# Staging places for the down units and the last two up units of a mixture-of-experts kernel, and up loads in pairs

## Chip, cores and metric
One core of a Trainium2 chip (trn2) runs one program. The metric is the time of one execution on the device in microseconds (us). The engines are TensorE (PE in the profile), VectorE (DVE), ScalarE (ACT), GpSimd (POOL) and SyncE (SP), which only issues DMAs; 16 DMA engines move the data.

## What is computed
One inference step of a decoder layer over 528 prompt rows (16 meta tokens and 512) and 8 sample rows of width 1024, float32: a gated linear attention group and a sliding-window attention group, their output projection, then a mixture of experts and a last RMS norm. The change is in the experts, cut to what matters:

```python
def moe_ffn(x2d, w_router, b_router, w_up, b_up, w_down, b_down):
    logits = (x2d @ w_router) + b_router                   # 520 tokens, 32 experts
    top_v, top_e = lax.top_k(logits, TOP_K)                # 4 experts per token
    gates = jax.nn.softmax(top_v, axis=-1)
    # tokens are grouped by expert and padded to whole blocks
    def expert_block(args):
        xb, e = args
        hh = xb @ w_up[e] + b_up[e]                        # (block, 1024) @ (1024, 2048)
        return clamped_swiglu(hh) @ w_down[e] + b_down[e]  # (block, 1024) @ (1024, 1024)
    # the results, times their gates, are added to each token
```

An expert's weights are 8 MB (up) and 4 MB (down). Every expert is read once.

## The kernel before
**Stages.** Until about 325 us the kernel projects, runs both attention groups and the router, and takes the products of the first block. The rest is the block loop and a tail that sums up each token's four expert outputs.

**Blocks.** Rows of one expert are cut into blocks of `SUB` = 64. With these inputs there are 46 blocks; 14 of the 32 experts have two, which stand one behind the other (blocks 0 and 1 are expert 0's). A table made on the chip orders the experts so that those with two blocks are spread, and holds for each block its expert and whether it is the expert's first (`is_new`).

**Units.** The weights come in units of 128 x 2048 float32 (1 MB): `UPU` = 8 for up, `DNU` = 4 for down. The tile `raw` has 12 places; unit j lies in place `SLOT[j]`, so there is one place for each unit of an expert. Four more places, `ahead`, take the first four ups of the second expert at the start; the region is work space otherwise.

**SyncE** issues all loads of weights in program order (lines 595 to 777). Before a unit's load it waits until TensorE has used that unit in the block before: `up_used` counts up units, `dn_used` down units. A load of a repeated block is issued with a false condition: nothing moves, its semaphore rises. In the loop over b from 4 (line 733) it issues the eight ups of block b (line 604) and then the four downs of block b - 1 (line 614). The loads of blocks 0, 2 and 3 are written out ahead of the loop (lines 674 to 731). Behind the loop come the last block's downs (line 747), then, once all but the last two blocks are scattered, `t_small` (line 741) and the eight `slot_pair` loads of the expert outputs (line 760).

**TensorE** does `up(b)` and then `down(b - 1)` (line 2317). `up_products` (line 2154) is four products per unit, two column halves by two banks; `down` (line 2273) the same for a down unit. At the start the order is written out: second_up (block 1), three units of third_up (block 2), down(0), one unit, down(1), `place` (which makes the lists of rows and outputs on TensorE), four units, then block 3.

**VectorE** clamps, forms SwiGLU and turns rows to columns with 32 x 32 transposes. Around 340 to 366 it makes `own_pos`, `dest`, `at_slot`, `at_block` and the lists from them, and then raises `lists_ready` (line 1537).

**ScalarE**, per block (line 1048), in order: `sigmoid(b)`, `seed_up(b + 1)` (the up biases into two PSUM banks), `hold(b + 2)` (gathered rows to `x_hold`), `y_out(b - 1)` (the down bank to `y_rows`), `seed_down(b)`. **GpSimd** gathers rows and scatters outputs by indirect DMAs.

**The tail.** TensorE's `small_slots` (line 2342) waits for `t_small`, then come `pair_rows` of four tiles, `rest_slots(2)`, `pair_rows(4)` and `rest_slots(4)` (line 2325), all in order. VectorE weighs the loaded slots (line 1756), adds TensorE's sums (line 1764) and multiplies by the gain `g_final_bc` (line 1744), which is loaded at line 731.

## Time and profile before
| what | us |
|---|---|
| median of 3 runs | 1339.25 (1336.02 to 1340.25) |
| span of the profiled execution | 1337.8 |
| TensorE busy (matmul) | 1283.2, 96% of the span |
| VectorE busy | 918.0, 69% |
| ScalarE busy | 285.1, 21% |
| SyncE's queue: moved | 441.56 MB, 81.2% of 16 engines' span |
| all DMA packets | 468.95 MB, mean 351 GB/s |

The profile is of one execution; times in it are microseconds from the first instruction. A matmul record counts as busy from its issue to a modelled end, so a TensorE that waits shortly between units still looks nearly full. The granted TensorE clock is 0.995 of 2.4 GHz in the mean, so nothing here is about the clock. A wait is given with what ended it. "PE ps L2159" is TensorE's work at line 2159 (a line of `up_products`) that writes PSUM.

### The profile page before, as it was taken

To read this page: it belongs to the slowest core of one execution; us is meant where nothing else is said; L and a number is where in the kernel's file an instruction comes from. 1 tells how busy PE (TensorE), PEld (TensorE's weight loads), DVE (VectorE), ACT (ScalarE), POOL (GpSimd) and SP (SyncE) were. 2 spreads that over 40 slices of the span, in tenths; PEclk is the share of its full clock that TensorE was granted. 3 is DMA by queue.
4 is the path that set the end of the run, shared out by engine and by line. 5 is a ranking of instruction groups with operands and counts; after the bars stand their busy time and mean duration, and the time that the engine had idled before them with its cause. 6 is when DMAs were issued, how large, how long until landed. Compare 5 with 4: busy or idle time off the path is not lost.

```text
span 1337.8 us, 21359 instructions
## 1 busy us (share of the span) xinstructions
PE 1283.2 (96%) x6323; PEld 520.2 (39%) x6323; DVE 918.0 (69%) x1877; ACT 285.1 (21%) x542; POOL 124.1 (9%) x229
## 2 busy tenths in 40 slices
PE   8999999999999999997999998899999997999996
PEld 6876565553333333332333332233333331333332
DVE  3215357656878777775787786687777875777778
ACT  4331143433112121111121121111121111121114
POOL 2000000000020110100110101010111100110100
PEclk9998999999999999999999999999999999999999
DMA  9405154078999999999999999999999999999996
GB/s 358 129 4 191 32 176 170 32 284 342 417 386 386 421 421 419 416 421 421 420 398 423 414 422 420 414 422 407 420 417 420 414 421 421 421 402 420 412 414 274
DMA packets 91409, 468.95 MB, mean 351 GB/s; under 512 B 11870, under 2 KB 29520, under 8 KB 41074
## 3 DMA queue, kind: packets, MB, share of 16 engines
q1 hardware_dynamic: 75070, 441.56, 81.2%
q0 software_dynamic: 7360, 16.79, 3.2%
q10 hardware_dynamic: 8948, 10.19, 2.2%
q8 instruction: 19, 0.31, 0.1%
q14 instruction: 12, 0.10, 0.0%
HBM read 614.82 MB, written 28.77 MB: 481 GB/s over the span
## 4 chain that ended last, share of the span: by engine, by line
PE 71%; DMA 21%; DVE 4%; SPq 2%; issue 1%; ACT 0%; DVEq 0%; POOL 0%; POOLq 0%; ACTq 0%
PE ps L2159 34%; DMA raw<-in_w_down_dram 19%; PE ps L2284 17%; PE ps L1845 5%; PE ps L1822 5%; PE ps L2060 3%; SPq L614 1%; DMA raw<-slot_outputs 1%; PE ps L2173 1%; DVE v_gate L1756 1%; DMA x_rows<-expert_inputs,row_idx 1%; PE ps L1924 0%; PE ps L2007 0%; PE ps L2015 0%; PE ps L2014 0%
## 5 line engine op out<-in xcount | busy, mean ns | idle before, releaser
L2159 PE MATMUL ps<-raw,xT 128*64 128x512 f32 x2816 | 617.4, 593 | 17.6 <-DMA raw<-in_w_up_dram 17.0
L1632 DVE STREAM_TRANSPOSE xT<-x_hold 32x192 f32<-32x192 f32 (+2 forms) x680 | 275.0, 404 | 154.1 <-PE ps L2159 133.9
L2159 PEld LDWEIGHTS ps<-raw,xT 128*64 128x64 f32 x2816 | 199.9, 137 | 424.6 <-issue 391.0
L2284 PE MATMUL ps<-raw,aT 128*64 128x512 f32 x1408 | 317.1, 595 | 16.7 <-DMA raw<-in_w_down_dram 16.7
L1632 DVE STREAM_TRANSPOSE aT<-act_g 32x256 f32<-32x256 f32 x352 | 223.5, 635 | 64.4 <-PE ps L2284 54.5
L2284 PEld LDWEIGHTS ps<-raw,aT 128*64 128x64 f32 x1408 | 97.6, 137 | 229.2 <-issue 174.7
L1016 ACT ACTIVATE act_s<-act_g 128x512 f32<-128x512 f32 x46 | 29.0, 630 | 632.6 <-DVE act_g L1616 632.6
L566 POOL DMA_INDIRECT slot_outputs<-y_rows,out_idx x44 | 45.2, 1028 | 609.3 <-ACT y_rows L1021 608.4
L1404 DVE STREAM_TRANSPOSE bias_up<-up_cols 128x1024 f32<-128x1024 f32 x46 | 57.3, 1245 | 1.6
L1845 PE MATMUL ps<-w_c_cols,hT 128*128 128x512 f32 x128 | 56.8, 596 | 0.0
L558 POOL DMA_INDIRECT x_rows<-expert_inputs,row_idx x47 | 49.3, 1049 | 71.2 <-issue 53.5
L1021 ACT ACTIVATE y_rows<-ps 128x512 f32<-128x512 f32 x45 | 26.9, 597 | 99.0 <-PE ps L2284 99.0
L2060 PE MATMUL ps<-w_out_sb,mixT 128*128 128x512 f32 x96 | 42.8, 599 | 0.1
L1012 ACT ACTIVATE x_hold<-x_rows 128x512 f32<-128x512 f32 x45 | 28.3, 630 | 59.6 <-DVE xT L1632 58.5
L1616 DVE TENSOR_SCALAR act_g<-ps 128x512 f32<-128x512 f32 x46 | 31.8, 692 | 10.8 <-PE ps L2159 9.5
L1822 PE MATMUL ps<-hT,w_a_cols 128*128 128x268 f32 x160 | 36.6, 390 | 0.0
L1845 PEld LDWEIGHTS ps<-w_c_cols,hT 128*128 128x128 f32 x128 | 23.7, 190 | 27.8 <-issue 27.8
L1623 DVE TENSOR_TENSOR act_g<-act_l,act_s 128x512 f32<-128x512 f32 x46 | 31.8, 692 | 1.6
L1621 DVE SCALAR_TENSOR_TENSOR act_l<-act_l,act_g 128x512 f32<-128x512 f32 x46 | 31.8, 692 | 1.4
L966 ACT ACTIVATE ps<-bias_up 128x512 f32<-128x512 f32 x47 | 28.3, 601 | 20.8 <-DVE bias_up L1404 13.8
L1822 PEld LDWEIGHTS ps<-hT,w_a_cols 128*128 128x128 f32 x160 | 30.3, 190 | 6.1 <-issue 0.4
L1617 DVE TENSOR_SCALAR act_l<-ps 128x512 f32<-128x512 f32 x46 | 31.3, 681 | 0.0
(405 smaller groups left out, 899.7 us busy)
## 6 DMA issues: line engine op xcount, KB each, us to landing
raw<-in_w_up_dram SPq DMA_DIRECT2D x356, 1024.0 KB
raw<-in_w_down_dram SPq DMA_DIRECT2D x180, 1024.0 KB, 10.5
slot_outputs<-zeros ACTq DMA_DIRECT2D x1, 8320.0 KB, 27.9
...
```

The lines of the kernel that those rows point to most:

```text
L558: pool.indirect_dma_start(x_rows[:], None, xn_halves, bass.IndirectOffsetOnAxis(ap=idx[:, 0:1], axis=0), bounds_check=last_row, oob_is_err ...
L566: pool.indirect_dma_start(slot_halves, bass.IndirectOffsetOnAxis(ap=out_idx[:, 0:1], axis=0), y_rows[:], None, bounds_check=last_out, oob_ ...
L1404: return dve.transpose(bias_up[:].rearrange("p a (c r) -> p (a c) r", r=32), bc(up_cols[:], 2, [P, 2 * COLS, 32]))
L1616: dve.tensor_scalar(act_g[:], ps[:, banks[0], :], LIMIT, None, ALU.min).then_inc(g_ready, 1)
L1621: o.do(dve.scalar_tensor_tensor(act_l[:], act_l[:], 1.0, act_g[:], ALU.add, ALU.mult))
L1623: dve.tensor_tensor(act_g[:], act_l[:], act_s[:], ALU.mult).then_inc(a_ready, 1)
L1632: dve.transpose(dst_at(rows_out, group), src_at(rows_in, parity)).then_inc(done, 1)
L1822: ins = mm(ps[:, n % 4, 0:HALF], w[:, k, c0:c0 + P], hT[:, k, half], start=(k == 0), stop=(k == KT - 1))
L1845: ins = mm(ps[:, bank, 0:n], hT[:, k, a:z], w[:, k, c0:c0 + n], start=(k == 0), stop=(k == KT - 1))
L2060: ins = mm(ps[0:r, 6 + n, :], mixT[:, k, 0:r], w_out_sb[:, k, 512 * n:512 * n + 512], start=(k == 0), stop=(k == KT - 1))
L2159: ins = mm(ps[SUB * i:SUB * i + SUB, banks[bank], :], rows_in[:, j, :], weights[:, c:c + HF], start=False, stop=(j == at_end), skip_group_ ...
L2284: ins = mm(ps[SUB * i:SUB * i + SUB, 2, :], aT[:, j, r, :], raw[:, units[j], D * r + HF * i:D * r + HF * i + HF], start=False, stop=(j == ...
```

## The change
- The places. There are 18 instead of 16: 12 low ones, and six high ones (`HIGH`) where other tiles lay. Each unit has a home (`UP_AT`, `DOWN_AT`); ups 6 and 7 and the four downs have a staging place too (`UP_STAGE_AT`, `DOWN_STAGE_AT`). Tiles of the stages before and of the tail move accordingly; `own_pos`, `dest`, `at_slot` and `at_block` now lie in `LATE0` to `HIGH1`, which are the staging places of downs 2 and 3.
- ScalarE gets `move_ups` (two copies of 128 x 2048 per block) and `move_downs` (four), each from the staging place to the home once TensorE has used the home's last content; for a repeated block the source is the home itself.
- SyncE loads a staged unit once its staging place is emptied (`up_moved`, `down_moved`), and ups 0 to 5 as before, once TensorE has used them. Ups are loaded in pairs of units, the staged pair first. The table has two rows more, from which SyncE takes the blocks to wait for (`block_ahead`, `previous_start`); `is_new` becomes a two-bit value.
- TensorE waits for a copy (`up_moved`, `down_moved`) instead of a landing for the staged units. Its order of work is the same, but for the order of units in the first three blocks and `up(3)`, `down(2)`, now inside the loop.
- At the start, the second expert's two staged ups and downs 0 and 1 are loaded ahead; its downs 2 and 3 after `lists_ready`; its home ups by `load_ups(2)`.
- At the end, the last block's downs are used from the staging places, and `t_small` and `g_final_bc` are loaded behind the eight slot loads.

The diff, cut to its core:

```diff
-AHEAD = 4
-BY_LANDING = list(range(AHEAD, UPU)) + list(range(AHEAD))
+BY_LANDING = [3, 2, 0, 1, 4, 5, 6, 7]
+STAGED = (UPU - 2, UPU - 1)
...
+        LOW = [RAW0 + UNIT * 4 * i for i in range(UPB)]
+        HIGH = [HIGH0 + UNIT * 4 * i for i in range(6)]
+        UP_AT = [HIGH[0], HIGH[1], LOW[10], LOW[11], LOW[0], LOW[1], LOW[2], LOW[3]]
+        UP_STAGE_AT = [LOW[5], LOW[6]]
+        DOWN_AT = [LOW[4], LOW[9], HIGH[2], HIGH[3]]
+        DOWN_STAGE_AT = [LOW[7], LOW[8], HIGH[4], HIGH[5]]
+        SLOTS_AT = UP_STAGE_AT + UP_AT[0:6]
...
+        def staged_or_home(stage, home, new):
+
+            low, step = min(stage, home) // 4, abs(stage - home) // 4
+            which = new if stage > home else 1 - new
+            return weights[:, low:low + 2 * step].rearrange("p (k s) -> p k s", k=2)[:, bass.ds(which, 1), 0:UNIT]
...
+        R = Region(LATE0, HIGH1)
         own_pos = R("own_pos", [P, NTILE, NE])
         dest = R("dest", [P, NTILE, TOPK])
         dest_slot = R("dest_slot", [P, NTILE, TOPK])
         dest_block = R("dest_block", [P, NTILE, TOPK])
...
+            def load_up_pair(e, j, cond):
+                at = UP_STAGE_AT[0] if j in STAGED else UP_AT[j]
+                sp.sem_inc(weights_asked, 1)
+                sp.dma_start(unit(at, 2), up_source(e, j, 2), cond=cond).then_inc(landed[j], 16)
...
-                    load_up(0, 0, None)
-                    load_up(0, 1, None)
+                    load_first(3)
+                    load_first_down(1)
                     sp.wait_ge(max_ready, PT)
-                    load_up(0, 2, None)
+                    load_first(2)
                     sp.wait_ge(pv_psum, PT)
-                    load_up(0, 3, None)
-                    for j in range(AHEAD):
-                        load_ahead(1, j, None)
+                    load_first(0)
+                    load_first(1)
+                    load_first_down(2)
+                    load_first_down(3)
+                    load_second(STAGED[0])
                     sp.wait_ge(mixT_psum, 2 * NTILE)
-                    load_up(0, 4, None)
+                    load_second(STAGED[1])
                     sp.wait_ge(out_psum, NTILE)
-                    for j in range(5, UPU):
-                        load_up(0, j, None)
+                    for j in range(4, UPU):
+                        load_first(j)
...
+            load_first_down(0)
             sp.wait_ge(part_psum, NTILE)
             sp.wait_ge(h2_stored, 16 * NTILE)
             sp.wait_ge(caches_stored, 2 * 16)
-            for j in range(2, DNU):
-                load_down(0, j, None)
+            load_second_down(0)
+            load_second_down(1)
...
+            def load_ups(b):
+                e_up, new = expert(sp, b), is_new(sp, b)
+                ahead, previous = block_ahead(sp, b), previous_start(sp, b)
+                sp.wait_ge(landed[STAGED[0]], 16 * b)
+                sp.sem_inc(weights_asked, 1)
+                sp.wait_ge(up_moved, 2 * previous + 2)
+                load_up_pair(e_up, STAGED[0], new // 2)
+                for j in range(0, STAGED[0], 2):
+                    sp.wait_ge(landed[j], 16 * b)
+                    sp.sem_inc(weights_asked, 1)
+                    sp.wait_ge(up_used, UPU * ahead + (j + 2))
+                    load_up_pair(e_up, j, new % 2)
+
             def load_downs(b):
-                e_dn, new_dn = expert(sp, b - 1), is_new(sp, b - 1)
+                e_dn, new, previous = expert(sp, b), is_new(sp, b), previous_start(sp, b)
                 for j in range(DNU):
-                    sp.wait_ge(dn_used, DNU * b + (j + 1))
-                    load_down(e_dn, j, new_dn)
+                    sp.wait_ge(landed[UPU + j], 16 * b)
+                    sp.sem_inc(weights_asked, 1)
+                    sp.wait_ge(down_moved, DNU * previous + (j + 1))
+                    load_down(e_dn, j, new // 2)
 
             sp.wait_ge(table_made, 1)
-            e_up, new_up = expert(sp, 2), is_new(sp, 2)
-            other = second_is_other(sp)
-            sp.wait_ge(ahead_landed, AHEAD_LANDED + 16 * AHEAD)
-            for n, j in enumerate(range(AHEAD, UPU)):
-                sp.wait_ge(up_used, UPU + n + 1)
-                load_up(e_up, j, new_up)
-                if n < AHEAD:
-                    sp.sem_inc(landed[n], 16)
-                    load_ahead(e_up, n, other)
-            e_up, new_up = expert(sp, 3), is_new(sp, 3)
-            for n, j in enumerate(range(AHEAD)):
-                sp.wait_ge(up_used, 2 * UPU - AHEAD + n + 1)
-                load_up(e_up, j, None)
-            for n, j in enumerate(range(AHEAD, UPU)):
-                sp.wait_ge(up_used, 2 * UPU + n + 1)
-                load_up(e_up, j, new_up)
-            load_downs(3)
-            sp.wait_ge(up_used, 3 * UPU)
-            sp.dma_start(g_final_bc[:], g_final.rearrange("(a n) -> a n", a=1).to_broadcast([P, D])).then_inc(ld_gfinal, 16)
             nb = block_count(sp)
+            sp.wait_ge(second_landed, SECOND_LANDED + 4 * 16)
+            load_ups(2)
+            sp.wait_ge(lists_ready, 1)
+            load_second_down(2)
+            load_second_down(3)
+            load_ups(3)
+            sp.wait_ge(second_landed, SECOND_LANDED + 6 * 16)
+            load_downs(2)
             with sp.Fori(4, nb) as b:
-                e_up, new_up = expert(sp, b), is_new(sp, b)
-                for j in range(UPU):
-                    sp.wait_ge(up_used, UPU * b + (j + 1 - UPU))
-                    load_up(e_up, j, new_up)
-                load_downs(b)
+                load_ups(b)
+                load_downs(b - 1)
...
             def load_last_down(e, j):
-                src = w_down[0, column(e)].rearrange("a (p c r) n -> c p (a r n)", c=DNU, r=2)[j]
-                sp.wait_ge(up_used, UPU * sent + (UPU + j + 1))
-                sp.dma_start(raw[:, LAST_DOWN[j], :], src).then_inc(last_down_landed[j], 16)
-
-            def unit_is_free(j):
-                if j < UPU:
-                    sp.wait_ge(up_used, UPU * sent + (UPU + j + 1))
-                else:
-                    sp.wait_ge(dn_used, DNU * nb + (j - UPU + 1))
+                sp.wait_ge(down_moved, DNU * ahead + (DNU + j + 1))
+                sp.dma_start(unit(DOWN_STAGE_AT[j]), down_source(e, j)).then_inc(last_down_landed[j], 16)
...
-            load_small()
             for n in range(len(SLOT_ORDER)):
                 load_slots(n)
+            sp.wait_ge(dn_used, DNU * sent + 3 * DNU)
+            load_small()
+            sp.dma_start(g_final_bc[:], g_final.rearrange("(a n) -> a n", a=1).to_broadcast([P, D])).then_inc(ld_gfinal, 16)
...
+            def move_ups(b):
+                new = is_new(act, b) % 2
+                act.wait_ge(landed[STAGED[0]], 16 * b + 16)
+                for i, j in enumerate(STAGED):
+                    act.wait_ge(up_used, UPU * b + (j + 1 - UPU))
+                    act.activation(unit(UP_AT[j]).unsqueeze(1), staged_or_home(UP_STAGE_AT[i], UP_AT[j], new),
+                                   ACT.Copy).then_inc(up_moved, 1)
+
+            def move_downs(b):
+                new = is_new(act, b) % 2
+                for j in range(DNU):
+                    act.wait_ge(landed[UPU + j], 16 * b + 16)
+                    act.wait_ge(dn_used, DNU * b + (DNU + j + 1))
+                    act.activation(unit(DOWN_AT[j]).unsqueeze(1), staged_or_home(DOWN_STAGE_AT[j], DOWN_AT[j], new),
+                                   ACT.Copy).then_inc(down_moved, 1)
+
             act.wait_ge(table_made, 1)
             nb = block_count(act)
             act.wait_ge(up_read, 2)
             seed_up(3, (0, 1))
+            move_ups(2)
+            y_out(1)
+            move_downs(2)
             sigmoid(2)
             act.wait_ge(up_read, 3)
+            seed_down(2)
+            move_ups(3)
             hold(4)
-            y_out(1)
-            seed_down(2)
-            with act.Fori(3, nb) as b:
+            last = scattered_blocks(act)
+            with act.Fori(3, last) as b:
                 sigmoid(b)
                 act.wait_ge(up_read, b + 1)
                 seed_up(b + 1, (0, 1))
+                move_ups(b + 1)
                 hold(b + 2)
                 y_out(b - 1)
                 seed_down(b)
+                move_downs(b)
...
+            def up_landed(j, b):
+                if j in STAGED:
+                    pe.wait_ge(up_moved, 2 * b + (j - STAGED[0] + 1))
+                elif j % 2 == 0:
+                    pe.wait_ge(landed[j], 16 * b + 16)
...
+            def down(b):
+                pe.wait_ge(down_seeded, b + 1)
+                pe.wait_ge(aT_ready, 8 * b + 8)
+                for j in range(DNU):
+                    pe.wait_ge(down_moved, DNU * b + (j + 1))
+                    down_products(j, aT, unit(DOWN_AT[j]))
...
+            third_up(range(0, 3))
+            first_down(0, aT)
+            third_up(range(3, 4))
+            first_down(1, aT_last)
             place()
-            third_up(BY_LANDING[4:])
+            third_up(range(4, UPU))
             pe.wait_ge(table_made, 1)
             nb = block_count(pe)
-            up(3)
-            down(2, aT, SLOT[UPU:])
-            with pe.Fori(4, nb) as b:
+            with pe.Fori(3, nb) as b:
                 up(b)
-                down(b - 1, aT, SLOT[UPU:])
+                down(b - 1)
             turn_small()
```

## Rows read from the trace of the kernel before

**Rows 1.** Page, section 2: GB/s in 40 slices of 33.4 us, whole span.
```profile
GB/s 358 129 4 191 32 176 170 32 284 342 417 386 386 421 421 419 416 421 421 420 398 423 414 422 420 414 422 407 420 417 420 414 421 421 421 402 420 412 414 274
```

**Rows 2.** Page, section 4: chain that ended last, by engine.
```profile
PE 71%; DMA 21%; DVE 4%; SPq 2%; issue 1%; ACT 0%; DVEq 0%; POOL 0%; POOLq 0%; ACTq 0%
```

**Rows 3.** Waits of TensorE: who waited for whom, us in total, times, longest.
```profile
PE ps L2159 <- DMA raw<-in_w_up_dram: 17.0, 24, 1.3
```

**Rows 4.** Timeline, TensorE, 616 to 680: start, us, operation, idle before and releaser.
```profile
618.96 1.94 PE L2159 MATMUL ps<-raw,xT 128*64 128x512 f32 x8 [0.56 <-DMA raw<-in_w_up_dram]
...
633.16 13.90 PE L2159 MATMUL ps<-raw,xT 128*64 128x512 f32 x64
...
653.76 13.90 PE L2159 MATMUL ps<-raw,xT 128*64 128x512 f32 x64
```

**Rows 5.** Windows: busy us of PE, PEld, DVE, ACT, POOL, PEclk, DMA share, GB/s.
```profile
320.00:340.00 20.00, 19.42 (x101) 7.58 (x103) 15.95 (x43) 5.89 (x12) 1.00 (x1) 1.00 0.75 289
370.00:380.00 10.00, 10.00 (x48) 3.31 (x46) 8.20 (x15) 2.35 (x4) 3.35 (x5) 1.00 0.82 306
405.00:420.00 15.00, 15.00 (x74) 5.01 (x72) 13.57 (x27) 3.58 (x6) 2.27 (x3) 1.00 0.90 340
420.00:1320.00 900.00, 865.59 (x3960) 280.12 (x3957) 675.19 (x1315) 154.72 (x262) 98.18 (x160) 1.00 1.01 417
690.00:705.00 15.00, 14.46 (x68) 4.44 (x66) 11.41 (x23) 3.58 (x6) 2.28 (x4) 1.00 0.96 372
1320.00:1325.00 5.00, 5.00 (x13) 2.25 (x12) 4.74 (x6) 2.87 (x5) 0.00 (x0) 1.00 0.22 92
```

**Rows 6.** Windows, the same columns: 4 KB rows (25:35), 8 KB rows (662:682).
```profile
25.00:35.00 10.00, 10.00 (x45) 8.21 (x44) 0.00 (x0) 5.63 (x8) 0.73 (x4) 1.00 1.02 422
662.00:682.00 20.00, 20.00 (x96) 6.67 (x94) 16.24 (x32) 3.58 (x6) 2.45 (x4) 1.00 1.01 420
```

**Rows 7.** Timeline, SyncE's queue, 327 to 344: start, us of issuing, load, count.
```profile
329.39 0.34 SPq L604 DMA_DIRECT2D raw<-in_w_up_dram  x1
...
335.74 6.12 SPq L601 DMA_DIRECT2D raw<-in_w_up_dram  x4
343.43 12.32 SPq L604 DMA_DIRECT2D raw<-in_w_up_dram  x4
```

**Rows 8.** Timeline, VectorE's lists and TensorE's first products of block 3.
```profile
364.37 0.23 DVE L1531 TENSOR_SCALAR lst<-ps 128x68 f32<-128x68 f32 x1 [0.75 <-PE ps L2210]
...
365.49 0.23 DVE L1536 SCALAR_TENSOR_TENSOR row_idx_all<-lst 128x68 int32<-128x68 f32 x1
...
371.02 2.32 PE L2159 MATMUL ps<-raw,xT 128*64 128x512 f32 x10
```

**Rows 9.** Groups of ScalarE by form: count, busy us, mean ns, idle before.
```profile
L1016 ACT ACTIVATE act_s<-act_g 128x512 f32<-128x512 f32 x46 | 29.0, 630 | 632.6 <-DVE act_g L1616 632.6
...
L1080 ACT ACTIVATE t_sq<-v_gate 128x1024 f32<-128x1024 f32 x4 | 4.2, 1057 | 6.0 <-DVEq L1765 4.0 <-DVEq L1759 2.0
```

**Rows 10.** SyncE's line 604, not-done loads, then done: ns min/median/max, first, last.
```profile
L604 SPq DMA_DIRECT2D raw<-in_w_up_dram x8: 73/73/88, 608.2 to 623.7; - x8
...
L604 SPq DMA_DIRECT2D raw<-in_w_up_dram x8: 332/333/346, 656.7 to 668.0; - x8
```

**Rows 11.** Timeline from 1291: SyncE, then TensorE, then VectorE of the tail.
```profile
1291.95 0.81 SPq L741 DMA_DIRECT2D t_small<-slot_outputs  x2
...
1312.61 1.04 PE L2346 MATMUL ps<-t_small,small_hitT 32*24 32x512 f32 x4
1313.97 7.44 PE L2337 MATMUL ps<-y_pair,t_hitT 128*128 128x512 f32 x16 [0.33 <-ACT y_pair L1070]
...
1324.68 3.60 PE L2330 MATMUL ps<-raw,t_diag 128*128 128x512 f32 x8
...
1330.43 1.22 DVE L1764 TENSOR_TENSOR v_gate<-ps,v_gate 128x1024 f32<-128x1024 f32 x1
...
1333.45 1.28 DVE L1744 SCALAR_TENSOR_TENSOR v_gate<-v_gate,t_stat,g_final_bc 128x1024 f32<-128x1024 f32 x1
```

282 lines of the change are left out of this document (151 added, 131 removed).

## The prediction

> **What bounds the kernel now.** I read the slices first: from the eleventh of 40 to the last but one the 16 DMA engines move 386 to 423 GB/s, mostly about 421 [rows 1]. The chain of waits then names TensorE for 71% of the span and DMA for 21% [rows 2], which looks like a TensorE kernel. The waits correct that: TensorE's up line waits 24 times for weights, 17.0 us in sum [rows 3], and the busy share hides more. Where TensorE is starved, a unit (1 MB, eight matmul records) starts every 2.49 us though it is busy 1.94; where it is not, blocks of 8 up and 4 down units start 20.60 us apart (633.16 and 653.76), 1.72 a unit [rows 4]. 1.049 MB in 2.49 us is 421 GB/s. So the block loop has two rates that lie close together. TensorE needs 20.6 us for a block; DMA needs 12 x 2.49 = 29.9 us for an expert. There are 46 blocks (the sigmoid runs 46 times [rows 9]) over 32 experts, so 14 blocks reuse their expert's weights; 43 blocks lie between the start of block 3 at 371.0 [rows 8] and the end, 22.1 us each. 43 x 20.6 = 886 us would fit into 926. **The bound is the stream of bytes**: with it at 417 GB/s over 900 us [rows 5], the time can only fall by filling holes in the stream, and rises by every new hole. All is reckoned as "where does the stream end": now at 1321.1 (the window 1320:1325 moves 92 GB/s, 1.1 us of full flow [rows 5]), where the last of the eight slot loads lands; the end of the span, 1337.8, is 16.7 us behind it.
>
> **Holes of now.** Against 421, window 320:340 (289) lacks 6.3 us, 370:380 (306) 2.7 and 405:420 (340) 2.9; 420:1320 (417) lacks 8.6, most of it in small dips where a repeated block holds the places, such as 690:705 (372, 1.7 us) [rows 5]. Sum 20.5 us: this is all that staging can win, since bytes stay the same.
>
> **Part 1, staging in the loop.** Before, a unit's load waits until TensorE has used the unit in the block before. After, six of twelve units land in a staging place that is free as soon as ScalarE has moved the last content, also during a repeat. In a full stream the next expert's first home pair is asked for after 4 downs, 4 downs and a staged pair (25 us), and TensorE needs 17 for what must be used by then (four up units, four downs, two ups of the repeat: 10 x 1.72). So the holes at 370:380 and 405:420 (5.6 us) go, and of the 8.6 us I take 5 (bounds 0 and 8.6: window 690:705 has a DMA share of 0.96, not of 0.88 as its bytes would have, so part of the loss is small gather and scatter packets, which stay [rows 5]).
>
> **Part 2, the copies.** Six per block, 128x2048, SBUF to SBUF, also for a repeat (home onto home). Nearest rows: 128x512 takes 630 ns, 128x1024 1057 ns, both SBUF to SBUF [rows 9], so 0.83 ns an element and 2048 give 1.91 us. Bounds: 1.9, and 2.5 if the address in a register or in-place reading costs as much as a whole small instruction. ScalarE has 3.58 us of work in a block now (six instructions in 662:682 [rows 6]); with 11.5 it has 15.1 of 20.6. The up copies lie behind the seeding of the next block, in the 6.9 us of down products; the down copies behind the seeding of the down bank, in the 13.7 us of the next up products. Queued behind them on ScalarE is the next sigmoid, for which VectorE waits, and then the seeds, for which TensorE waits. If downs land late, ScalarE stands in `move_downs`, and seeds come some 1 to 2 us after the last down product instead of before it. That makes TensorE late, not the stream: cost 0, covered by the 40 us that TensorE has over. SyncE's extra register loads and waits (about 2 us a block) have the same cover; a load that is not done holds SyncE for only 73 ns against 332 [rows 10], so repeats pass through.
>
> **Part 3, loads in pairs.** Rows of 16 KB where there were 8 KB, and 2 MB per load. Is the stream faster? The `w_c_cols` load has rows of 4 KB and its window 25:35 runs at 422; the 8 KB rows in 662:682 run at 420 [rows 6]. Doubling the row brought nothing there, so I take 0 (bounds: 1% either way on the some 600 us of up loads that remain, 6 us). The Trainium skill ("DMA: Bandwidth & Descriptors", section Why small descriptors are slow) gives a fixed overhead of about 3 cycles per packet, beside 256 cycles for 8 KB. By it the up loads would win an estimated 0.6%, some 3.5 us; the two windows show nothing of it.
>
> **Part 4, the start, where the change loses.** Both kernels ask for 16 units before the block table is made, at nearly the same times. Before, SyncE then feeds the stream without a pause: block 2's last four ups from 327.4 (the second at 329.39), block 3's first four from 335.74, its others from 343.43, and then block 2's downs [rows 7]. After, block 2's staged ups and two downs are there already; its six home units come in pairs as units 1, 3 and 5 of block 1 are used, the first at 329.4, the last near 337. With a microsecond from issue to flow (an estimate) they move from 330.5 to 345.5. Then **SyncE stands at `lists_ready`**, because downs 2 and 3 of the second expert land where `own_pos`, `at_slot` and `at_block` lie until the lists are made, and block 3's eight ups, free to load, are queued behind it. VectorE ends the lists at 365.7; it idled 0.75 us before their first row [rows 8]. The table gets some seven small operations more, of about 0.2 us like the lists' own, 1.3 us in sum; less the 0.75 that is 366.3. Flow starts at 367.8. Holes: 323.2 to 330.5 is 7.3, 345.5 to 367.8 is 22.3, in sum 29.6, against 6.3 in 320:340 now. Block 3's first pair lands after two downs, the staged pair and itself, at 367.8 + 6 x 2.49 = 382.7; TensorE, ready at 371.0 [rows 8], stands 12 us. From there on the stream is full: SyncE's next wait, for `move_ups(3)` (behind four down copies that start near 376, the sigmoid, a seed and itself, 7.6 + 1.2 + 3.8), ends near 389, and the stream has work until 392.
>
> **Part 5, the tail.** The final gain vector and the small slots are loaded behind the eight slot loads instead of at 371 and at 1291.95 [rows 11]. That takes 0.66 MB out of the stream before its measured end: -1.5 us. But `small_slots` is the first of TensorE's last products, and all that follows stands behind it. Now it starts at 1312.61, 8.5 us before the stream ends; the four pair products follow at 1313.97 for 7.44, the last `rest_slots` runs 1324.68 for 3.60 [rows 11]. After, it starts when `t_small` has landed, 1.5 us behind the slots (bounds 0.5 and 3: completion of a small load). From its start to the end of the last product it is 1324.68 + 3.60 - 1312.61 = 15.7, then from VectorE's add 1330.43 to its last product's end 1333.45 + 1.28 = 1334.7 another 4.3 [rows 11], and 3.1 to the end of the span. VectorE alone comes to about the same: it has three tiles done, then tile 3 (5.2), norm, two adds, two norms, add; I take 0.2 more. Sum 1.5 + 15.7 + 4.3 + 3.1 + 0.2 = 24.8 behind the stream's end, where it is 16.7 now: **+8.1**. The loads of the last downs and slots have their places earlier than now; that is worth nothing in a full stream.
>
> **Sum.** New holes 29.6, old ones gone 6.3 + 5.6 + 5 = 16.9, moved bytes 1.5: the stream ends 11.2 later, at 1332.3. Plus 24.8: a span of 1357.1. The median of the runs shown lies 1.45 over this span (1339.25 to 1337.8), so **1358.5**, some 19 us or 1.4% slower.
>
> **Rivals.**
> (a) *The hole at the lists is filled*, and the kernel ends on the other side. If SyncE's wait were over by 345.5, the sum is 7.3 - 16.9 - 1.5 = -11.1, and with the tail's +8.1 it is 1336. It needs lists 20 us sooner; for it speaks only that TensorE's products before them could move, against it that `place` starts behind both first down blocks in the new order too. If the tail also has slack, 1328.
> (b) *The wide rows pay.* The up loads that remain are 30 experts x 8 units x 2.49 = 598 us. From 3.2% on (434 GB/s) the 19.3 us are paid back; at half of that it gives 1349. Against it: the 4 KB and 8 KB windows [rows 6]. The same page's section Where 436 GB/s comes from puts the ceiling at 435; by that this rival can reach no change at best, 1339.
> (c) *The copies become the bound.* ScalarE's block would have to exceed the 22.1 us that a block takes, so a copy over (22.1 - 3.6 - 1.5)/6 = 2.8 us. At 3.0 us each, 43 blocks cost about 1.0 us more each: 1400 with the rest. Against it: 0.83 ns an element in both rows [rows 9].
> (d) *The change doesn't keep the stream full*: SyncE waits in order, also for a landing of twelve units before, so that the old dips stay or new ones come at each repeat (14 x 0.5 us). It gives 1358.5 + 5 + 7 = 1370.5.
> (e) *The tail is as now*, because the small load lands sooner than queue order says: 1350.4.
>
> **Chances.** Forecast with (e) and its own bounds, 1349 to 1366: 0.68. (d) 0.10, (c) 0.03, (b) 0.07, (a) 0.12, of which 0.07 faster and 0.05 no change. A measurement of this kernel can tell 0.3%, 4 us, from no change. Faster 0.10 (something for (a) and (b) together), same 0.08, slower 0.82. Range: from 1338, which leaves most of (a) and all of (c) out, to 1371.
>
> **What would show it.** Windows 345:368 near zero GB/s and SyncE waiting for VectorE there; block 3 starting near 383; 421 GB/s from 369 to the end with no dips at repeats; copies of 1.9 us; the first product on `t_small` behind the last slot landing, near 1334. Wrong if the stream flows at 350, if up loads run above 430, if ScalarE's copies are what TensorE waits for in the middle of the loop, or if the stream shows holes after 400.

## The result and the profile after

The changed kernel takes **1357.74 us** (median of 4 runs, 1355.95 to 1359.27), against 1339.75 for the one before: a ratio of 1.0141, 95% interval 1.0124 to 1.0159. It is slower by 1.4%. The profiled execution has a span of 1354.2 us.

The slices of the page of the changed kernel (40 of 33.9 us; the clock in tenths of full speed, GB/s) answer to [rows 1]:

```profile
PEclk9999999999979999998999998999999998999998
GB/s 357 124 4 189 32 237 105 32 348 294 165 428 420 429 415 426 417 424 425 418 423 420 416 421 426 412 426 424 424 420 423 420 428 418 427 410 430 413 421 159
```

From the twelfth slice to the last but one none is below 410 GB/s, where before had slices at 386, 398, 402 and 407, and many are above the 423 that was the best of before. The eleventh is at 165, where before had 417. Windows of the same trace (busy us and count of PE, PEld, DVE, ACT and POOL, then PEclk, DMA share, GB/s), which answer to [rows 5]:

```profile
320.00:345.00 25.00, 22.84 (x115) 8.23 (x113) 20.11 (x52) 7.16 (x14) 1.99 (x2) 1.00 0.69 275
345.00:368.00 23.00, 23.00 (x180) 9.29 (x178) 19.20 (x38) 5.91 (x7) 0.18 (x1) 1.00 0.16 57
368.00:380.00 12.00, 3.91 (x20) 1.02 (x16) 1.98 (x3) 4.29 (x4) 3.48 (x5) 0.75 1.00 412
380.00:400.00 20.00, 13.88 (x52) 4.63 (x54) 8.56 (x14) 9.36 (x8) 1.43 (x3) 0.72 1.01 428
420.00:1320.00 900.00, 873.43 (x4022) 288.47 (x4020) 685.41 (x1341) 602.63 (x512) 100.45 (x163) 0.99 1.01 421
1324.00:1326.00 2.00, 0.00 (x0) 0.00 (x0) 1.73 (x2) 0.00 (x0) 0.00 (x0) 1.00 1.04 431
1326.00:1327.00 1.00, 0.00 (x0) 0.00 (x0) 0.00 (x0) 0.00 (x0) 0.00 (x0) 0.71 1.00 293
1327.00:1328.00 1.00, 0.00 (x0) 0.00 (x0) 0.00 (x0) 0.00 (x0) 0.00 (x0) 0.50 0.91 324
```

The loop runs at 421 GB/s where it ran at 417. A hole is counted, as in the prediction, as the time that the missing bytes would take at 421 GB/s. The 23 us from 345 to 368 move 57 GB/s: that is a hole of 19.9 us of full flow. Full flow ends at about 1326.3, where only the small loads are left. What SyncE stood for, from the waits of its queue (us in sum, times, longest) and its timeline (start, us of issuing, load, count; answers to [rows 7]):

```profile
SPq L641 <- DVEq L1608: 28.4, 1, 28.4
SPq L645 <- ACT weights L1084: 7.3, 1, 7.3
...
327.73 10.41 SPq L646 DMA_DIRECT2D weights<-in_w_up_dram  x4
366.52 0.95 SPq L641 DMA_DIRECT2D weights<-in_w_down_dram  x2
370.29 2.84 SPq L646 DMA_DIRECT2D weights<-in_w_up_dram  x4
```

It asks for nothing between 338 and 366.5, and DVEq L1608 is the raise of `lists_ready`. TensorE's timeline shows what block 3 and the tail paid (start, us, operation, and in brackets the idle time before and its releaser; answers to [rows 8] and [rows 11]):

```profile
385.91 9.68 PE L2235 MATMUL ps<-weights,xT 128*64 128x512 f32 x32 [14.00 <-DMA weights<-in_w_up_dram]
...
1329.12 1.90 PE L2437 MATMUL ps<-t_small,small_hitT 32*24 32x512 f32 x4 [7.82 <-DMA t_small<-slot_outputs]
1330.95 8.56 PE L2428 MATMUL ps<-y_pair,t_hitT 128*128 128x512 f32 x16
1339.35 1.88 PE L2421 MATMUL ps<-weights,t_diag 128*128 128x512 f32 x4
1341.06 1.88 PE L2428 MATMUL ps<-y_pair,t_hitT 128*128 128x512 f32 x4
1342.78 3.60 PE L2421 MATMUL ps<-weights,t_diag 128*128 128x512 f32 x8
```

And the copies, from the page's groups (count, busy us, mean ns, idle before and what ended most of it):

```profile
L1092 ACT ACTIVATE weights<-weights 128x2048 f32 x172 | 319.6, 1903 | 178.0 <-DMA weights<-in_w_down_dram 165.6
L1084 ACT ACTIVATE weights<-weights 128x2048 f32 x88 | 162.6, 1895 | 4.6 <-DMA weights<-in_w_up_dram 4.6
```

A copy takes 1.90 us. ScalarE stands 178.0 us before the down copies, nearly all of it for landings, and 4.6 us before the up copies; TensorE, by the same page, stands 4.1 us for down copies. Who else waits for a copy is SyncE, before it may load the staging place again; e7_up_copies_twice below turns on that.

### The profile page after: what moved, and what is told of

Its sections match the earlier page's. It is cut to its first block, busy times and chain, and to the rows that moved or that the text cites. A ratio compares the mean times of both kernels' runs of the same rounds, so it can differ in the third digit from the quotient of the medians.

```text
span 1354.2 us, 22946 instructions
## 1 busy us (share of the span) xinstructions
PE 1285.6 (95%) x6323; PEld 525.4 (39%) x6323; DVE 920.9 (68%) x1885; ACT 751.2 (55%) x803; POOL 124.1 (9%) x229
## 4 chain that ended last, share of the span: by engine, by line
PE 69%; DMA 21%; DVE 3%; SPq 2%; ACT 2%; issue 2%; ACTq 0%; DVEq 0%; POOL 0%; POOLq 0%
PE ps L2235 35%; PE ps L2357 16%; DMA weights<-in_w_down_dram 12%; DMA weights<-in_w_up_dram 6%; PE ps L1921 5%; PE ps L1898 5%; PE ps L2136 3%; ACT weights L1092 2%; DMA t_small<-slot_outputs 1%; DMA x_rows<-expert_inputs,row_idx 1%; DMA w_a_cols<-in_w_in_dram 1%; DMA expert_inputs<-h 1%; SPq L650 1%; PE ps L2000 0%; PE ps L2083 0%
## 5 line engine op out<-in xcount | busy, mean ns | idle before, releaser
L2235 PE MATMUL ps<-weights,xT 128*64 128x512 f32 x2816 | 622.9, 600 | 36.8 <-DMA weights<-in_w_up_dram 36.2
L1092 ACT ACTIVATE weights<-weights 128x2048 f32 x172 | 319.6, 1903 | 178.0 <-DMA weights<-in_w_down_dram 165.6
L2235 PEld LDWEIGHTS ps<-weights,xT 128*64 128x64 f32 x2816 | 203.6, 139 | 445.7 <-issue 429.1
L2357 PE MATMUL ps<-weights,aT 128*64 128x512 f32 x1408 | 313.2, 593 | 4.3 <-ACT weights L1092 4.1
L1708 DVE STREAM_TRANSPOSE aT<-act_g 32x256 f32<-32x256 f32 x352 | 224.2, 637 | 37.9 <-PE ps L2357 27.9
L2357 PEld LDWEIGHTS ps<-weights,aT 128*64 128x64 f32 x1408 | 99.5, 137 | 210.5 <-issue 184.8
L1084 ACT ACTIVATE weights<-weights 128x2048 f32 x88 | 162.6, 1895 | 4.6 <-DMA weights<-in_w_up_dram 4.6
L1003 ACT ACTIVATE ps<-bias_up 128x512 f32<-128x512 f32 x47 | 27.9, 595 | 20.0 <-DVE bias_up L1474 13.6
L1898 PEld LDWEIGHTS ps<-hT,w_a_cols 128*128 128x128 f32 x160 | 30.3, 190 | 6.1 <-issue 0.4
```

Source lines behind the costliest of these rows:

```text
L1084: act.activation(unit(UP_AT[j]).unsqueeze(1), staged_or_home(UP_STAGE_AT[i], UP_AT[j], new), ACT.Copy).then_inc(up_moved, 1)
L1092: act.activation(unit(DOWN_AT[j]).unsqueeze(1), staged_or_home(DOWN_STAGE_AT[j], DOWN_AT[j], new), ACT.Copy).then_inc(down_moved, 1)
L1708: dve.transpose(dst_at(rows_out, group), src_at(rows_in, parity)).then_inc(done, 1)
L1898: ins = mm(ps[:, n % 4, 0:HALF], w[:, k, c0:c0 + P], hT[:, k, half], start=(k == 0), stop=(k == KT - 1))
L2235: ins = mm(ps[SUB * i:SUB * i + SUB, banks[bank], :], rows_in[:, j, :], w[:, c:c + HF], start=False, stop=(j == UPU - 1), skip_group_check ...
L2357: ins = mm(ps[SUB * i:SUB * i + SUB, 2, :], rows_in[:, j, r, :], w[:, c:c + HF], start=False, stop=(j == DNU - 1 and r == 1), skip_group_c ...
```

## The experiments

The theory is the prediction's: the stream of bytes is the bound, and the new time is the hole at the lists and a longer tail. The kernel before, run beside the first four, took 1338.3 us. The changed kernel was measured beside 1339.75; differences to it are differences of medians, and taken by the ratios they come out up to 1 us otherwise.

### e1_fill: nothing that is free waits behind the lists

SyncE asks for block 3's staged pair and its first two home pairs ahead of the wait for the lists, and ScalarE's copies of block 2's staged ups, which empty the place for that pair, go ahead of what waited for later work.

```diff
+            load_ups(3, late_downs)   # after two home pairs: wait lists_ready, then downs 2 and 3
...
             act.wait_ge(table_made, 1)
+            move_ups(2)
+            y_out(0)
...
             seed_up(3, (0, 1))
-            move_ups(2)
             y_out(1)
-            move_downs(2)
             sigmoid(2)
...
             move_ups(3)
             hold(4)
+            move_downs(2)
```

> The changed kernel with another order at the start and nothing else: ScalarE moves block 2's staged ups right after the sigmoid of block 1 and block 2's downs after move_ups(3), and SyncE issues block 3's staged pair and first two home pairs ahead of its wait for the lists; only the last home pair stays behind it. Theory 1 (the hole in the stream of bytes at the lists, 345 to 367 in the changed kernel, costs its full length): three pairs (15 us of stream) move into the hole, a hole of 5 us stays before the lists and some 2 us elsewhere; the stream ends about 14 us earlier, at 1313, and the time is 1344 (1341 to 1347), against 1358 of the changed kernel. Rival (the loop has cover for the hole, the loss sits in the copies or the tail): 1356 to 1359. Second rival (the half clock of TensorE behind its 14 us of idling is part of the loss): more than 14 us are won, 1340 or less.

Measured: **1348.59 us**, ratio 1.008 (1.0063 to 1.0097), 9.1 less than the changed kernel. Windows of e1_fill, the columns as above, and ScalarE's timeline:

```profile
345.00:360.00 15.00, 15.00 (x74) 5.01 (x72) 13.79 (x25) 4.41 (x5) 0.00 (x0) 1.00 0.93 375
360.00:370.00 10.00, 10.00 (x119) 4.87 (x117) 5.41 (x14) 1.12 (x2) 1.40 (x3) 1.00 0.68 265
380.00:385.00 5.00, 4.72 (x22) 1.62 (x24) 4.77 (x8) 5.00 (x4) 0.84 (x3) 1.00 0.24 56
...
377.55 0.60 ACT L1063 ACTIVATE y_rows<-ps 128x512 f32<-128x512 f32 x1 [12.61 <-POOLq L614]
379.33 3.71 ACT L1085 ACTIVATE weights<-weights 128x2048 f32 x2 [0.17 <-issue]
```

Summed from 320 to 400 the holes are 19.3 us here (8.7 in 320:345, 329 GB/s in 345:368, 382 in 368:380, 327 in 380:400) against 28.6 in the changed kernel: 9.3 less, and the time fell by 9.1. Most of the hole is filled, but a new one stands at 380:385. ScalarE stood 12.6 us in block 1's output copy, for GpSimd's permission to overwrite `y_rows` (line 614, behind the first scatters, which need the lists); behind it was the copy that frees the staged place for block 4.

### e2_tail: the small loads on a queue of their own

```diff
-            sp.wait_ge(dn_used, DNU * sent + 3 * DNU)
-            load_small()
-            sp.dma_start(g_final_bc[:], ...)
...
             seed_down(last)
+            act.wait_ge(scattered, 16 * sent)
+            act.dma_start(t_small[...], slot_dram[...])   # two halves
+            act.dma_start(g_final_bc[:], ...)
```

> The changed kernel with the loads of the small slots and of the final gain vector taken from SyncE's queue, where they stand behind the eight slot loads, and issued on ScalarE's queue once the last but one down block is done. Theory 1 (the tail costs what lies behind the last slot load): t_small lands before the last down products end near 1321, small_slots starts there and not at 1329, TensorE keeps its full clock, and the distance from the end of the stream to the end of the span falls from 27.3 back to about 17: 1347 (1345 to 1350). Rival (the landing of the last slots sets the tail in any case): 1356. Theory 1 has the clock in the windows behind 1325 at 1.00 again; it was 0.64 there.

Measured: **1350.15 us**, ratio 1.0084 (1.0067 to 1.01), 7.6 less. TensorE's timeline of e2_tail:

```profile
1319.75 7.09 PE L2355 MATMUL ps<-weights,aT_last 128*64 128x512 f32 x32 [0.34 <-ACT ps L1036]
1327.10 1.04 PE L2435 MATMUL ps<-t_small,small_hitT 32*24 32x512 f32 x4 [0.26 <-DMA t_small<-slot_outputs]
1328.14 7.44 PE L2426 MATMUL ps<-y_pair,t_hitT 128*128 128x512 f32 x16
```

`small_slots` follows the last down with a wait of 0.26 us in place of 7.82: the predicted 8.1 us of part 5 are there (7.6 measured), and were the loads' place in SyncE's order. The span ends 18.0 us behind the stream's end (1334.1, from the window 1332:1336 at 219 GB/s) where it was 27.9, as expected. The time missed its 1347 by 3 us all the same: the 0.66 MB of the small loads, 1.6 us of flow, now lie before the stream's end again, which the expectation left out; the rest is not assigned. This profile is of the slowest of the four runs, and its lists were ready only at about 370.9.

### e3_fill_tail: both

> Both edits, the fill of the hole at the start and the small loads on ScalarE's queue. If the two losses are independent, as theory 1 has it, they add: 1358 - 14 - 10.6 = 1333 (1330 to 1337), which is 0.5% faster than the kernel before. If one hides behind the other: 1344 or more.

Measured: **1340.19 us** (10 runs), ratio 1.0012 (1.0002 to 1.0021), 17.5 less than the changed kernel. The two effects add up (9.1 + 7.6 = 16.7), so the two losses are separate, and together they are nearly all of the 18.0 us. It misses the expected 1333 by 7 us: the two parts missed theirs by 4.9 (14 expected, 9.1 won) and 3.0 (10.6 and 7.6). The new hole seen in e1_fill is here too, 186 GB/s in 380:390, 5.6 us.

### e4_single_ups: how much is the width of the rows?

The changed kernel with each pair loaded as two units, rows of 8 KB as in the kernel before. Each unit has its own semaphore, and the engines wait for it.

```diff
-                sp.dma_start(unit(at, 2), up_source(e, j, 2), cond=cond).then_inc(landed[j], 16)
+                for k in range(2):
+                    sp.dma_start(unit(at + UNIT * 4 * k), up_source(e, j + k, 1), cond=cond).then_inc(landed[j + k], 16)
```

> The changed kernel with each pair of up units loaded by two loads of 1 MB (rows of 8 KB in place of 16 KB), each with its semaphore, at the same moments; places, copies and waits stay. Theory W (wide rows pay): SyncE's queue took 79.3% of 1354.2 us = 1074 us of the engines for 441.55 MB in the changed kernel and 81.2% of 1337.8 = 1086 us in the kernel before, so singles cost 12 us: 1370 (1366 to 1373). Theory of the prediction (the row length is worth nothing, the difference comes from the queue that never runs short): 1358. What lies between tells how much of the 12 us is the row length.

Measured: **1367.26 us**, ratio 1.0218 (1.0201 to 1.0235), 9.5 more than the changed kernel, within what was expected if wide rows pay (1366 to 1373). Its loop, in the same columns, and one stretch of it, first here and then in the changed kernel:

```profile
420.00:1320.00 900.00, 870.36 (x3980) 282.91 (x3977) 676.65 (x1331) 596.95 (x501) 100.54 (x163) 0.99 1.01 418
662.00:682.00 20.00, 20.00 (x96) 6.75 (x94) 15.77 (x32) 15.08 (x13) 2.64 (x5) 1.00 1.01 422
662.00:682.00 20.00, 20.00 (x96) 6.75 (x94) 15.77 (x32) 14.29 (x12) 2.63 (x5) 1.00 1.01 429
```

418 GB/s against 421 with pairs and 417 in the kernel before: staging alone won about 2 us of the loop (900 x 1/417), the pairs about 6.4 (900 x 3/421), and the rest of the 9.5 lies outside that window. The windows are rounded to 1 GB/s, so each of these two is good to some 2 us. The DMA engines are as busy in both kernels (share 1.01) and the rate differs, 422 against 429 where the kernel before had 420 [rows 6], so it is not a queue that runs short. What this doesn't separate is the length of a row from the size of a load, since both double.

### e5_order: the new wait on ScalarE out of the way

On e3_fill_tail, block 2's sigmoid and block 3's staged copies go ahead of block 1's output copy. The kernel before, run beside it, took 1339.25.

```diff
             seed_up(3, (0, 1))
-            y_out(1)
             sigmoid(2)
+            move_ups(3)
+            y_out(1)
             act.wait_ge(up_read, 3)
             seed_down(2)
-            move_ups(3)
```

> The kernel with the start reordered and the tail's small load on ScalarE's queue, and one more step: on ScalarE the sigmoid of block 2 and the two staged-up copies of block 3 go ahead of the output copy of block 1, which in e3_fill_tail waits 12.7 us for GpSimd's permission. Theory (the stream's holes set the time): the load of block 4's staged pair is released near 380.5 instead of 387.6, the hole at 380:390 (186 GB/s, 5.6 us of flow) goes, the tail stays: 1335, within 2 us, just faster than the kernel before. Rival (that hole is SyncE's or a landing's, not ScalarE's): 1340 as in e3_fill_tail.

Measured: **1337.61 us** (12 runs), ratio 0.9993 (0.9981 to 1.0005); against e3_fill_tail by the ratios 0.19% less, 2.5 us. The copies now run at 372.91 and ScalarE waits 0.26 us for GpSimd where it stood 12.66:

```profile
372.91 3.71 ACT L1077 ACTIVATE weights<-weights 128x2048 f32 x2
376.88 0.60 ACT L1055 ACTIVATE y_rows<-ps 128x512 f32<-128x512 f32 x1 [0.26 <-POOLq L614]
```

But the windows 360:370 (274 GB/s) and 380:390 (319) still lack 5.9 us. Half the step, as expected in kind and not in size: block 4's staged pair is asked for at 381.21, though its copies are done at 376.6. SyncE waited 4.8 us for the landing of downs 2 and 3 before that (SPq L470, see e12_ups_first).

### e10_lists_alone and e6_early_lists: the lists sooner

TensorE's `place()` ahead of `first_down(1)`, VectorE's `lists()` ahead of `turn_fourth()`. In e10_lists_alone this is done in the changed kernel, in e6_early_lists in e5_order. The kernel before, run beside them, took 1338.34.

```diff
+            place()
             first_down(1, aT_last)
-            place()
...
                 placements(k)
+            lists()
 
             turn_fourth()
             dve.wait_ge(aT_ready, 16)
             stage(own, 2)
-            lists()
```

> The changed kernel with the lists made earlier and nothing else. In it SyncE is free for the lists' wait at 338 and the queue is dry at about 347; the lists end at 366.4 and 345:368 moves 57 GB/s. Made earlier they end near 360, so flow starts 6 us sooner: 1357.7 - 6 = 1352. Rival (the wait is not what opens the hole): 1358.

> e5_order, and the lists made earlier: TensorE's products that place the slots go ahead of the down products of block 1, and VectorE makes the lists ahead of turning block 3's rows. In e5_order the last input of those products is ready at 356.1 and they run from 361.97 to 364.5, the lists end at 365.9. Theory (SyncE's wait for the lists opens the holes of 345:390): lists at 359.6, the two downs asked for before the queue is dry, so that the 3.5 us that 360:370 lacks (274 GB/s) go, and of the 1.3 and 2.4 of 370:380 and 380:390 about 2: 1337.6 - 5.5 = 1332. Rival (a): what comes behind is late instead (block 3's rows, turned 3 us later, or GpSimd), and it stays at 1336 to 1338.

Measured: e10_lists_alone **1357.25 us**, ratio 1.014 (1.0125 to 1.0156), no change from the changed kernel. e6_early_lists **1336.46 us** (11 runs), ratio 0.9985 (0.9976 to 0.9994). e6_early_lists was expected at 1332 and gave its rival's number: against e5_order (0.9993) the intervals overlap. Its window 360:370 is full now (419 GB/s for 274), and 380:390 has 179 for 319; the hole has moved. e10_lists_alone is the rival's number too, though not for the rival's reason. Its SyncE, its ScalarE and its windows:

```profile
361.81 0.81 SPq L641 DMA_DIRECT2D weights<-in_w_down_dram  x2
374.08 2.85 SPq L646 DMA_DIRECT2D weights<-in_w_up_dram  x4
...
368.92 0.60 ACT L1003 ACTIVATE ps<-bias_up 128x512 f32<-128x512 f32 x1 [10.78 <-DVE bias_up L1474]
369.97 3.69 ACT L1084 ACTIVATE weights<-weights 128x2048 f32 x2
...
360.00:370.00 10.00, 10.00 (x58) 3.47 (x56) 8.42 (x18) 1.08 (x3) 2.46 (x4) 1.00 0.69 258
370.00:380.00 10.00, 4.37 (x20) 0.97 (x16) 1.98 (x3) 4.39 (x5) 1.20 (x2) 1.00 0.51 188
```

The two downs are asked for 4.7 us sooner, and then SyncE stands again, until 373.7, for the staged copies of block 2 on ScalarE. These stand behind the seeding of block 3, which waits for VectorE, and VectorE now waits 1.6 us for TensorE's products and makes the lists first. In the changed kernel the same copies end at 364.89 + 3.69 = 368.6 and the pair behind them is asked for at 370.29, so even with the copies where they were the pair could have come only some 1.5 us sooner (an estimate from these two times). **Behind the wait that the profile named there was a second that ended 2 us later**, and hidden by the first. This edit takes the first away and moves the second later, and is worth nothing; the first taken away with the copies in place was not run, and by the estimate could win some 2 us. e1_fill takes both away, and wins 9 us. (This execution ran 2.1 us behind the changed kernel's at its first paired load, 329.83 against 327.73.)

### e12_ups_first: one more wait

On e6_early_lists, block 2's last four up units go ahead of block 1's down products. The kernel before, run beside it, took 1338.79.

```diff
             place()
+            third_up(range(4, UPU))
             first_down(1, aT_last)
-            third_up(range(4, UPU))
```

> e6_early_lists, and on TensorE the last four up units of block 2 go ahead of the down products of block 1. In e6_early_lists SyncE asks for block 3's third pair at 374.0, when those units are used, and for block 4's staged pair at 385.5, behind the staged copies of block 3 (378.6 to 382.4), so the queue is dry from about 380 and 380:390 moves 179 GB/s (5.7 us of flow). Theory (each hole of the start is held by one wait, and this is the last of them): both requests come 7 us sooner, the hole goes, 1336.5 - 5 = 1331.5, and the kernel is faster than the one before by 0.5%. Rival (the next wait is as late: the output copy of block 1 now comes 7 us later, and with it the down seed and GpSimd's scatters): 1336 as in e6_early_lists, with the hole moved on past 390.

Measured: **1336.15 us** (11 runs, 1332.9 to 1338.57), ratio 0.9981 (0.9969 to 0.9992): as e6_early_lists, within what can be told. The staged copies of block 3 are done at 372.8 now, but the queue is dry from 376 to 382:

```profile
SPq L470 <- DMA weights<-in_w_down_dram: 10.6, 1, 10.6
...
370.00:376.00 6.00, 6.00 (x30) 2.01 (x28) 3.75 (x7) 4.62 (x6) 1.40 (x3) 1.00 1.03 435
376.00:382.00 6.00, 6.00 (x30) 2.01 (x28) 3.78 (x7) 6.00 (x4) 1.23 (x2) 1.00 0.11 38
```

SyncE stands 10.6 us until the second expert's last downs have *landed*, before it issues block 2's not-done down loads; block 4's staged pair, whose place is free, is queued behind and is asked for at 381.17. When the awaited landing came, at about 375.4, the queue had only some 1 us of flow left. This wait was 1.0 us in the changed kernel, 4.8 in e5_order and 3.4 in e6_early_lists. Taking it away was not tried; by these windows it would be worth some 5 us, an estimate (6 us at 38 GB/s).

### e7_up_copies_twice, e8_all_copies_twice: how much cover has ScalarE?

Each copied unit is copied once more, onto itself, in e7_up_copies_twice the two ups only, in e8_all_copies_twice all six.

```diff
-                                   ACT.Copy).then_inc(up_moved, 1)
+                                   ACT.Copy).then_inc(soft_ready, 1)
+                    act.wait_ge(soft_ready, 2 * b + (i - 2))
+                    act.activation(unit(UP_AT[j]), unit(UP_AT[j]), ACT.Copy).then_inc(up_moved, 1)
```

> The changed kernel with each of the two staged up units of a block copied once more, onto itself, before it is handed on: ScalarE gets some 3.8 us more per block, 18.9 in all from the prediction's 15.1. Prediction's cover (TensorE's block takes 20.6 us and a block of the stream 22.1): no change, 1358, at most 1361. Rival (the copies lie on the path from landing to use or from use to the next load): 1.9 to 3.8 us for each of 43 blocks, 1440 to 1520.

> The changed kernel with all six staged units copied once more onto themselves: ScalarE's block goes from 15.1 to 26.5 us, over the 22.1 that a block takes. Prediction's rival (c), that ScalarE becomes the bound once its block exceeds 22.1: 43 x 4.4 = 189 us more, 1547, TensorE waiting for the copies all through the loop and the stream well under 421 GB/s. Rival (the threshold is elsewhere, since only 29 of the 43 blocks bring loads and the others are short): above 1547 if what counts is 20.6 in repeats and 29.9 in new experts: then only repeats and runs of blocks of one expert pay, some 14 x 6 = 84 us, 1442.

Measured: e8_all_copies_twice **1565.88 us**, ratio 1.1697 (1.1675 to 1.172), 208 us more than the changed kernel, 4.8 for each of 43 blocks where 4.4 were expected: the bound by ScalarE is as the rival (c) has it. Its loop, 346 GB/s with ScalarE busy 192.60 of 200 us, and TensorE's down products, which wait 168.9 us for it:

```profile
820.00:1020.00 200.00, 162.38 (x734) 49.88 (x730) 126.39 (x248) 192.60 (x136) 19.65 (x32) 1.00 0.85 346
L2361 PE MATMUL ps<-weights,aT 128*64 128x512 f32 x1088 | 261.8, 602 | 168.9 <-ACT weights L1097 168.9
```

But e7_up_copies_twice takes **1381.54 us**, ratio 1.0326 (1.0304 to 1.0347), 24 us more, where the prediction's cover gives none and its rival 80 to 160. Both are wrong. SyncE's waits in the loop, then its timeline and two windows at a repeated block:

```profile
SPq L645 <- ACT weights L1087: 95.0, 15, 6.8
...
448.10 1.76 SPq L650 DMA_DIRECT2D weights<-in_w_down_dram  x4
459.81 5.87 SPq L646 DMA_DIRECT2D weights<-in_w_up_dram  x4
...
455.00:460.00 5.00, 5.00 (x26) 1.65 (x24) 4.75 (x9) 4.97 (x5) 0.00 (x0) 1.00 0.87 374
460.00:465.00 5.00, 5.00 (x26) 1.56 (x24) 2.02 (x4) 4.55 (x4) 2.27 (x3) 1.00 0.91 311
```

In the changed kernel that wait (SPq L645 on ACT weights L1084, in the same stretch) is 30.3 us, 15 times, longest 2.3, and the two issues at the same place start at 444.43 and 452.16, 7.7 us apart; four downs are 10.0 us of flow, so the queue never runs dry. With 3.8 us more on ScalarE they are 11.7 us apart, and it does: 1.7 us each by these times. The loop runs at 412 GB/s for 421, which is 19 of the 24 us, 1.3 for each of 15 such places; another 3 are in 368:400, where the changed kernel lacks nothing. So the cover of a copy is not the idle time of its engine per block (TensorE's 20.6 less ScalarE's 15.1); it is what is still in the queue when the load behind the copy is asked for, here 2.3 us (10.0 less 7.7, an estimate from one place).

### e11_down_pairs: the down units in pairs too

e6_early_lists with the four downs of the loop loaded as two pairs, in rows of 16 KB.

```diff
-                for j in range(DNU):
+                for j in range(0, DNU, 2):
                     sp.wait_ge(landed[UPU + j], 16 * b)
                     sp.sem_inc(weights_asked, 1)
-                    sp.wait_ge(down_moved, DNU * previous + (j + 1))
-                    load_down(e_dn, j, new // 2)
+                    sp.wait_ge(down_moved, DNU * previous + (j + 2))
+                    load_down_pair(e_dn, j, new // 2)
```

> e6_early_lists with the down units of the loop also loaded in pairs, 16 KB rows in place of 8 KB. In e4_single_ups the up units' rows of 16 KB were worth 9.5 us for 240 units (8 per expert), 1.6% of their time. Theory (the rate of the stream goes by row length): 29 experts x 4 units x 2.49 = 289 us at 1.6% is 4.6 us less than e6_early_lists, 1327 to 1328. Rival (a pair waits for two free places, and the copies come in two bursts, so the queue runs dry at repeats): 0 to 5 us more than e6_early_lists.

Measured: **1371.77 us**, ratio 1.0253 (1.0239 to 1.0267), 35 us more than e6_early_lists, where at most 5 were expected. The loop falls to 405 GB/s:

```profile
420.00:1320.00 900.00, 848.94 (x3866) 271.89 (x3864) 656.63 (x1288) 577.44 (x487) 100.55 (x163) 0.99 0.98 405
SPq L650 <- ACT weights L1087: 112.7, 30, 3.8
```

A pair is asked for when both its places are moved, and a copy is free to start when both units have landed: SyncE's longest wait for a down copy grows from 2.1 us to 3.8, and that for the staged ups behind them from 2.3 to 3.3. SyncE's wait for down landings grows from 4.1 us to 39.9. This looks like the small cover of e7_up_copies_twice again; the cause is read from the waits, and no run takes it apart. 900 x 16/421 = 34 us: all of the loss is in the loop, and the wider rows, expected at 4.6, can't be seen beside it.

### e9_tail_clock: is it the clock?

In the tail of the changed kernel the products on `t_small` and `y_pair` take 1.90 and 8.56 us where before they took 1.04 and 7.44. The experiment puts products into a PSUM bank that is overwritten later, for the time in which TensorE waits for `t_small`.

```diff
             pe.wait_ge(hitT_copied, 8)
+            for j in range(DNU):   # 32 products, 64 records
+                ...mm(ps[..., 5, :], aT_last[:, j, r, :], w[:, c:c + HF], start=True, stop=True)
             small_slots()
```

> The changed kernel with 32 products more on TensorE after the last down units, into a PSUM bank that is overwritten later, so that TensorE has 7.0 us of work in the 7.8 us in which it waits for t_small. In the changed kernel the granted clock was 0.64 to 0.68 after that wait and the first product took 1.90 us, the next sixteen 8.56. Theory (the clock fell because TensorE stood): clock 1.00 there, 1.04 and 7.44 us, the end 2.0 us nearer to the landing of t_small. Rival (these products are slow for another reason, such as arriving data): 1.90 and 8.56 as before.

Measured: one time, 1359.51 us. A product is two records, so the filling took 14.0 us and not 7.0, and the tail began 5.6 us late; the total says nothing. The products behind it do:

```profile
1320.78 13.96 PE L2447 MATMUL ps<-weights,aT_last 128*64 128x512 f32 x64
1334.67 1.04 PE L2437 MATMUL ps<-t_small,small_hitT 32*24 32x512 f32 x4
1335.64 7.44 PE L2428 MATMUL ps<-y_pair,t_hitT 128*128 128x512 f32 x16
```

1.04 and 7.44 us again. From the first of them to the end of the span it is 23.1 us (1357.8 - 1334.67) where the changed kernel has 25.1 (1354.2 - 1329.12): 2.0 us of the tail were the clock. That data were arriving is not the reason: in e2_tail the same products take 1.04 and 7.44 with the stream at 410 GB/s in 1327:1328.

## Why the prediction was right, step by step

It gave 1358.5 and the time is 1357.7. The mechanism was right: the stream is the bound, and a hole at the lists and a longer tail are the loss; e3_fill_tail takes both away and with them 17.5 of the 18.0 us. That the number is within 1 us is luck: the sum hides terms that were off and cancelled.

**Bound.** Right: in e4_single_ups, e7_up_copies_twice and e11_down_pairs the stream's loss in the loop (6.4, 19 and 34 us) is most of what the time loses (9.5, 24 and 35), and e8_all_copies_twice shows the point where ScalarE takes over.

**The hole at the lists.** Predicted 345.5 to 367.8, 22.3 us; measured 19.9 us in 345:368. The first hole, predicted at 7.3, measures 8.7 in 320:345. Lists at 366.4 (forecast 366.3), the first product of block 3 at 385.91 (forecast 382.7). By the GB/s of the windows the bytes of the six units had moved by about 383, as forecast, and the landing came 3 us later; for the two downs the same lag shows (bytes by about 373.3, SyncE's wait for their landing over at 376.3). Its cause is open. SyncE's next wait ends at 389.26, as forecast (389). It named the hole's size rightly and its cause by half: e10_lists_alone shows that the lists alone are worth nothing, since the wait for `move_ups(2)` ends hardly later. Rival (a), "the wait is over by 345.5: 1336", would not have come from the lists alone either.

**Old holes.** Predicted: 5 of the loop's 8.6 us go, by staging. Measured: 8.6, 417 to 421 GB/s; not that nothing is lost any more, since 421 is no longer full flow where ups are loaded (429 in 662:682). The step's cause was wrong: e4_single_ups gives staging about 2 and the wide rows 6.4.

**Wide rows.** Predicted 0 with bounds of 6 either way; measured 9.5 us. The step that failed is the reading of [rows 6]: from "4 KB rows 422, 8 KB rows 420" it concluded that 16 KB bring nothing. No row of before has 16 KB rows, the two windows are of different loads and stages, and their difference of 0.5% is not small against the effect sought (9.5 of 598 us of up loads, 1.6%). In the changed kernel a window full of up loads reads:

```profile
455.00:460.00 5.00, 5.00 (x26) 1.72 (x24) 3.82 (x7) 5.00 (x4) 1.05 (x1) 1.00 1.01 432
```

Up loads above 430 were on the prediction's list of signs that it is wrong, and on this term it was. The Trainium skill ("DMA: Bandwidth & Descriptors", section Why small descriptors are slow) has a fixed cost per packet, by which the prediction had an estimated 3.5 us: the sign is confirmed, the size is nearly three times that. Rival (b) was half true: the rows did pay, and a time of 1349 did not follow, since without them it would have been 1367.

**Stream's end.** Of the windows' sums: 8.7 + 19.9 + 0.3 in 368:380 less 0.3 in 380:400 is 28.6 us of holes, forecast 29.6 + 3.6 = 33.2; before, 20.5. Less the moved bytes it should end 6.6 later; it ends at 1326.3, 5.2 later, forecast 11.2. The 1.4 left over are not assigned; in kernels with the same code up to there the first paired load is issued between 326.3 and 330.1.

**Tail.** Forecast 24.8 behind the stream's end; measured 1354.2 - 1326.3 = 27.9: `t_small` is used 2.8 us behind the slots (forecast 1.5, bounds 0.5 and 3; the small loads run at 293 GB/s), then 17.3 to the end of the last product where 15.7 were summed, and 7.8 where the sum has 7.6: 25.1 for 23.3. e9_tail_clock, at full clock, has 23.1, so 2.0 are the clock and the rest of the sum was right to 0.2. The clock was not thought of ("nothing here is about the clock" holds for the kernel before): the sum took durations from a stretch in which TensorE had been busy.

So 6.0 us too much for the stream and 3.1 too little for the tail: a span of 1354.2 where 1357.1 was forecast; the median lies 3.5 above this profile where 1.45 was added.

**Copies.** 1.90 us each, 1.91 forecast, cost 0: right at this size. The reason given (TensorE's 40 us to spare, 20.6 against 15.1; the 926 us behind the 40 are not worked out there) is wrong, as e7_up_copies_twice shows. At 2.5 us a copy, the upper bound that the prediction let pass as free, six copies would add 3.6 us to ScalarE's block, more than the 2.3; whether that would have been paid was not run.

**Rivals (d) and (e).** No slice of the loop is below 410 GB/s (d fell); `t_small` landed behind the slots (e fell).

**A version that beats both.** e12_ups_first, at 0.9981 of the kernel before (0.9969 to 0.9992), and e6_early_lists at 0.9985 are faster than both kernels, by 2 to 3 us over the one before, with intervals that leave out 1 and that overlap each other. That is less than 0.3%: what staging and wide rows win in the stream, some 14 us of old holes, the start gives back through one wait after another (the lists, ScalarE's order, a landing).
